# A MoE decoder kernel: the experts' pairs staggered by one and two stages on TensorE

## What is computed

```
scores = sigmoid(x @ router_w)                    # 64 experts
idx    = top 8 experts of each token, out of its 4 best groups
gate   = scores[idx] / sum * 2.5
for e in 64 experts:                              # D = 1024, hidden = 256
    xb = x[tokens of e]
    hb = silu(xb @ w_gate[e]) * (xb @ w_up[e])
    y[tokens of e] += (hb @ w_down[e]) * gate
y += (silu(x @ s_gate) * (x @ s_up)) @ s_down     # shared expert
x  = layer_norm(alpha * x + y)
```

## Time and profile before

| | us |
|---|---|
| median of 3 runs | 1343.61 (1341.33 to 1345.3) |
| profiled execution, its own time | 1345.01 |
| its span in the profile | 1343.2 |
| PE busy | 1307.0 (97%) |
| DVE busy | 421.1 (31%) |
| ACT busy | 307.3 (23%) |
| POOL busy | 28.1 (2%) |
| up projection L420, busy | 450.5, 2048 instructions |
| down projection L482, busy | 226.5, 992 instructions |

### The profile page before, as it was taken

How to read it: one execution, slowest core, us unless ns; L and a number is a source line. 1 busy time by engine, 2 the same in 40 slices (tenths; PEclk the granted TensorE clock), 3 DMA queues, 4 the chain that set the end, 5 groups by cost and what they waited for, 6 DMA issues and landing times.

```text
span 1343.2 us, 15738 instructions
## 1 busy us (share of the span) xinstructions
PE 1307.0 (97%) x6237; PEld 657.3 (49%) x6237; DVE 421.1 (31%) x903; ACT 307.3 (23%) x666; POOL 28.1 (2%) x101
## 2 busy tenths in 40 slices
PE   7999999999999999999989999999999999999996
PEld 5877854343443434344336655434434343444432
DVE  2767265212121211212133656421212112121213
ACT  3354331121121111111111343111211111111112
POOL 1004000000000000000000000000000000000000
PEclk9999999999999999999999998999999999999998
DMA  9306056789999999999983618588999999999991
GB/s 340 130 15 246 1 205 274 320 329 436 411 439 412 434 424 425 437 412 435 421 313 142 251 63 345 213 319 338 429 424 435 414 428 431 414 431 420 433 418 80
DMA packets 40581, 446.24 MB, mean 332 GB/s; under 512 B 5928, under 2 KB 8411, under 8 KB 23131
## 3 DMA queue, kind: packets, MB, share of 16 engines
q1 hardware_dynamic: 40006, 445.23, 80.0%
q10 hardware_dynamic: 532, 0.43, 0.1%
HBM read 444.60 MB, written 1.05 MB: 332 GB/s over the span
## 4 chain that ended last, share of the span: by engine, by line
PE 95%; DVE 2%; ACT 1%; issue 0%; DMA 0%; SPq 0%; DVEq 0%
PE psum L420 33%; PE psum L482 17%; PE psum L474 10%; PE psum L433 9%; PE psum L2047 4%; PE psum L2189 4%; PE psum L1167 3%; PE psum L574 2%; PE psum L1610 2%; PE psum L459 1%; PE psum L2195 1%; PE psum L1456 1%; PE psum L1206 1%; PE psum L607 1%; PE psum L466 1%; PE psum L568 1%
## 5 line engine op out<-in xcount | busy, mean ns | idle before, releaser
L420 PE MATMUL psum<-w_up_ring,moe_x_selected 128*64 128x512 f32 x2048 | 450.5, 592 | 0.0
L420 PEld LDWEIGHTS psum<-w_up_ring,moe_x_selected 128*64 128x64 f32 x2048 | 146.8, 137 | 290.4 <-issue 290.4
L482 PE MATMUL psum<-w_down_ring,moe_hT 128*64 128x512 f32 x992 | 226.5, 598 | 0.0
L1017 DVE SCALAR_TENSOR_TENSOR moe_h<-moe_silu,moe_slot_gate,psum 128x256 f32<-128x256 f32 x64 | 30.8, 480 | 381.3 <-ACT moe_silu L784 381.3
L482 PEld LDWEIGHTS psum<-w_down_ring,moe_hT 128*64 128x64 f32 x992 | 65.7, 136 | 128.5 <-issue 128.3
L784 ACT ACTIVATE moe_silu<-psum 128x256 f32<-128x256 f32 x64 | 24.7, 385 | 405.9 <-PE psum L420 405.9
L1022 DVE TENSOR_TENSOR moe_out_low<-psum,moe_out_high 128x512 fp32r<-128x512 f32 x64 | 44.3, 692 | 232.5 <-ACT moe_out_high L796 232.5
L474 PE MATMUL psum<-moe_out_high,moe_matchT 128*128 128x512 f32 x256 | 113.8, 444 | 0.0
L433 PE MATMUL psum<-moe_match,moe_x_high 128*128 128x448 f32 x256 | 102.3, 400 | 0.0
L474 PE MATMUL psum<-moe_out_low,moe_matchT 128*128 128x512 f32 x256 | 101.4, 396 | 0.0
L433 PE MATMUL psum<-moe_match,moe_x_low 128*128 128x448 f32 x256 | 93.2, 364 | 0.0
(11 more groups left out here) (500 smaller groups left out, 1124.7 us busy)
## 6 DMA issues: line engine op xcount, KB each, us to landing
w_up_ring<-in_moe_up SPq DMA_DIRECT2D x60, 4096.0 KB, 15.1
w_down_ring<-in_moe_down SPq DMA_DIRECT2D x62, 2048.0 KB, 13.2
w_up_ring<-in_moe_up SPq DMA_DIRECT2D x8, 2048.0 KB, 11.4
w_up_ring<-in_ev_w_in SPq DMA_DIRECT2D x4, 2048.0 KB, 13.2
w_up_ring<-in_od_w_in SPq DMA_DIRECT2D x4, 2048.0 KB, 12.7
w_up_ring<-in_ev_w_out SPq DMA_DIRECT2D x2, 2048.0 KB, 8.0
moe_shared_weights<-in_shared_up SPq DMA_DIRECT2D x2, 2048.0 KB, 7.7
moe_w_down_extra<-in_moe_down SPq DMA_DIRECT2D x2, 2048.0 KB, 18.0
```

What stands on the lines that cost most here:

```text
L420: last = nc.tensor.matmul(k.psum[e * SLOTS:(e + 1) * SLOTS, 6, :], xsel[:, kk, own:own + SLOTS], up_view(slots[e], kk), start=kk == 0, sto ...
L482: last = nc.tensor.matmul(k.psum[e * SLOTS:(e + 1) * SLOTS, bank, :], hT[:, j * P + e * SLOTS:j * P + (e + 1) * SLOTS], places[e][:, j, ha ...
```

## The change

The stage of pair p on TensorE becomes: up of pair p; match turn if i is 0 or 2; gather if i is 3; the whole combine of pair p-2 (8 matmuls in one row); down of pair p-1; turn of pair p. The transposes write PSUM bank 5 in place of bank 7. ACT and DVE read the down projection's result one stage later too (`take_high(p - 1)`, `take_low(p - 1)`). The down weights are asked for in the order of their new use. In `first_two_pairs` the shared expert's transposes go to bank 3 and no longer wait for `low`; the combine of pair 0 and the down of pair 1 move into the stage of pair 2. At the end the combine of pair 30 and the down of pair 31 are added after the last stage, and both parts of the shared expert's last product stand before the combine of pair 31. The matmuls are the same in number and shape. The overflow path (taken only when an expert has more than 56 tokens) keeps its own order, with its transposes still in bank 7; its hunk is left out below.

```diff
-    def pe_turn():
+    def pe_turn(bank=5):
 
         for j in range(KF):
-            last = nc.tensor.transpose(turn_ps[:, j * P:(j + 1) * P], h[:, j * P:(j + 1) * P], k.ident[:])
+            last = nc.tensor.transpose(k.psum[:, bank, j * P:(j + 1) * P], h[:, j * P:(j + 1) * P], k.ident[:])
...
-        def refill_down(p, i, par, freed):
+        def refill_down(pair, par, freed):
             sp.wait_ge(s.down_b, freed)
-            load_down_pair(sp, k.w_down_both[:, 2 * par:2 * par + 2], d, layer, 2 * i + par, dn[par])
...
         refill_up(2, 1, 0)
         refill_up(3, 1, 1)
-        refill_down(3, 1, 1, 2)
+        refill_down(4, 0, 1)
         refill_up(4, 2, 0)
-        refill_down(4, 2, 0, 1)
+        refill_down(3, 1, 2)
         refill_up(5, 2, 1)
-        refill_down(5, 2, 1, 4)
         with sp.Fori(3, PAIRS // 2) as i:
-            for par in range(2):
-                refill_up(2 * i + par, i, par)
-                refill_down(2 * i + par, i, par, 2 * i + par - 1)
+            refill_up(2 * i, i, 0)
+            refill_down(2 * i - 1, 1, 2 * i - 2)
+            refill_up(2 * i + 1, i, 1)
+            refill_down(2 * i, 0, 2 * i - 1)
+        refill_down(PAIRS - 1, 1, PAIRS - 2)
...
             shared_up(1, range(2, KD)).then_inc(s.shared_up, 1)
+            pe.wait_ge(s.turned_sb, 1)
             pe_turn_match((0, 1)).then_inc(s.match_turned, 1)
-            pe.wait_ge(s.turned_sb, 1)
             pe.wait_ge(dn[0], 16)
             pe_down(k.w_down[0:2], 0, 4).then_inc(s.down_a, 1)
             pe_down(k.w_down[0:2], 1, 7).then_inc(s.down_b, 1)
             pe.wait_ge(s.shared_h, NT)
-            pe.wait_ge(s.low_a, 1)
-            pe.wait_ge(s.low_b, 1)
-            pe.wait_ge(s.matchT, 1)
             for t in range(NT):
                 for j in range(KF):
-                    last = nc.tensor.transpose(k.psum[:, 4, (t * KF + j) * P:(t * KF + j + 1) * P],
+                    last = nc.tensor.transpose(k.psum[:, 3, (t * KF + j) * P:(t * KF + j + 1) * P],
                                                sh[:, t, j * P:(j + 1) * P], k.ident[:])
             last.then_inc(s.shared_hT_psum, 1)
-            pe_combine(0, 0, begin=True)
-            pe_turn_match((2, 3)).then_inc(s.match_turned, 1)
             pe.wait_ge(s.h, 2)
+            pe.wait_ge(s.matchT, 1)
             pe_turn().then_inc(s.turned, 1)
-            pe_combine(0, 1, begin=True).then_inc(s.combined, 1)
-            pe.wait_ge(s.turned_sb, 2)
-            pe.wait_ge(dn[1], 16)
-            pe.wait_ge(s.shared_hT, 1)
-            pe_down(k.w_down[2:4], 0, 4).then_inc(s.down_a, 1)
-            pe_down(k.w_down[2:4], 1, 7).then_inc(s.down_b, 1)
 
         def pair(q, i, first=False, final=False):
 
-            p, par = 4 * q + i, i % 2
-            slots, turn = (2 * par, 2 * par + 1), 2 * q + i // 2
+
+            p, par, turn = 4 * q + i, i % 2, 2 * q + i // 2
+            slots = (2 * par, 2 * par + 1)
             if i == 0:
                 pe.wait_ge(s.xsel_a, 4 * q + 3)
                 pe.wait_ge(s.xsel_b, 4 * q + 3)
             pe.wait_ge(gu[par], 16 * (turn + 1) + 16)
             pe.wait_ge(s.h, p)
             pe_up(slots, i, 4 * q + 4 if i == 0 else None).then_inc(s.up, 1)
-            pe.wait_ge(s.low_a, p)
-            pe.wait_ge(s.low_b, p)
-            pe.wait_ge(s.matchT, 2 * q + (i + 1) // 2)
+            pe.wait_ge(s.turned_sb, p)
+            if i % 2 == 0:
+                pe_turn_match((i, i + 1)).then_inc(s.match_turned, 1)
+            pe.wait_ge(s.low_a, p - 1)
+            pe.wait_ge(s.low_b, p - 1)
             if i == 3 and not final:
                 pe.wait_ge(s.match, NT * (q + 1) + 1)
                 pe_gather(4 * (q + 1), NT * (q + 2))
                 pe.wait_ge(s.quad_gates, q + 2)
                 pe.wait_ge(s.match_bf, q + 2)
                 pe_slot_gates().then_inc(s.slot_gates, 1)
-            pe_combine((i - 1) % 4, 0)
-            if i < 2:
-                pe_turn_match((2 * i, 2 * i + 1)).then_inc(s.match_turned, 1)
-            pe.wait_ge(s.h, p + 1)
-            if i == 3 and not final:
-                pe.wait_ge(s.gates_read, q + 2)
-            pe_turn().then_inc(s.turned, 1)
-            pe_combine((i - 1) % 4, 1).then_inc(s.combined, 1)
-            if first and i == 2:
+            pe.wait_ge(s.matchT, 2 * q + i // 2)
+            begin = first and i == 2
+            if begin:
+                pe.wait_ge(s.shared_hT, 1)
+            pe_combine((i - 2) % 4, 0, begin=begin)
+            pe_combine((i - 2) % 4, 1, begin=begin).then_inc(s.combined, 1)
+            if first and i == 3:
                 pe.wait_ge(s.shared_wd, 16)
                 shared_down(0, 0)
                 shared_down(0, 1)
-            pe.wait_ge(s.turned_sb, p + 1)
-            if first and i == 2:
-                down_places = extra_down
+                places = extra_down
                 pe.wait_ge(x.dn_extra, 16)
             else:
-                down_places = [k.w_down[slot] for slot in slots]
-                pe.wait_ge(dn[par], 16 * (turn + 1) if par else 16 * turn)
+                places = k.w_down[2 - 2 * par:4 - 2 * par]
+                pe.wait_ge(dn[1 - par], 16 * (2 * q + i // 2))
             if i == 3 and not final:
                 pe.wait_ge(s.xsel_a, 4 * q + 8)
-            pe_down(down_places, 0, 4).then_inc(s.down_a, 1)
-            pe_down(down_places, 1, 7).then_inc(s.down_b, 1)
+            pe_down(places, 0, 4).then_inc(s.down_a, 1)
+            if i == 3 and not final:
+                pe.wait_ge(s.gates_read, q + 2)
+            pe_down(places, 1, 7).then_inc(s.down_b, 1)
+            pe.wait_ge(s.h, p + 1)
+            if i % 2 == 0:
+                pe.wait_ge(s.matchT, turn + 1)
+            if i == 3 and not final:
+                pe.wait_ge(s.xsel_b, 4 * q + 8)
+            pe_turn().then_inc(s.turned, 1)
 
         first_two_pairs()
         for i in range(2, 4):
...
         n_over = pe.value_load(k.over_dram[0:1, 2:3], min_val=0, max_val=MAX_OVER)
         pair(QUADS - 1, 3, final=True)
         shared_down(1, 0)
+        pe.wait_ge(s.low_a, PAIRS - 1)
+        pe.wait_ge(s.low_b, PAIRS - 1)
+        pe_combine(2, 0)
+        pe_combine(2, 1).then_inc(s.combined, 1)
+        pe.wait_ge(s.turned_sb, PAIRS)
+        pe.wait_ge(dn[1], 16 * (PAIRS // 2))
+        pe_down(k.w_down[2:4], 0, 4).then_inc(s.down_a, 1)
+        pe_down(k.w_down[2:4], 1, 7).then_inc(s.down_b, 1)
+        shared_down(1, 1)
         pe.wait_ge(s.low_a, PAIRS)
         pe.wait_ge(s.low_b, PAIRS)
         with pe.If(n_over < 1):
             for t in range(NT):
-                if t == 1:
-                    shared_down(1, 1)
                 for half in range(2):
                     pe_combine(3, t, (half,)).then_inc(s.y_ready, 1)
 
...
             take_silu(p)
             if i == 3 and not final:
                 take_selected(4 * (q + 1))
+            if i % 2 == 0:
+                take_match(q, i // 2)
+            take_high(p - 1)
             take_turned(p)
-            if i < 2:
-                take_match(q, i)
-            take_high(p)
 
         take_silu(0)
         shared_silu(0)
...
         act.wait_ge(s.table_sb, 1)
         act.dma_start(k.over_dram, table_i[:]).then_inc(s.table_dram, 16)
         take_turned(1)
-        take_match(0, 1)
-        take_high(1)
...
                 dve.wait_ge(s.slot_gates, q + 2)
                 dve.wait_ge(s.h, p + 1)
                 read_slot_gates()
-            take_low(p)
+            take_low(p - 1)
 
         gated_h(0, 0)
         shared_h(0)
...
         shared_h(1)
         take_low(0)
         dve.wait_ge(s.shared_hT_psum, 1)
-        nc.vector.tensor_copy(shT[:].rearrange("p t j c -> p (t j c)"), k.psum[:, 4, :]).then_inc(s.shared_hT, 1)
-        take_low(1)
+        nc.vector.tensor_copy(shT[:].rearrange("p t j c -> p (t j c)"), k.psum[:, 3, :]).then_inc(s.shared_hT, 1)
...
                 pair(q, i)
         for i in range(4):
             pair(QUADS - 1, i, final=True)
+        take_low(PAIRS - 1)
```

More of the change, by code:

```diff
@@ L510, in sync @@
         load_down_pair(sp, extra_down_both[:], d, layer, 2, x.dn_extra)
-        def refill_down(p, i, par, freed):
+        def refill_down(pair, par, freed):
             sp.wait_ge(s.down_b, freed)
-            load_down_pair(sp, k.w_down_both[:, 2 * par:2 * par + 2], d, layer, 2 * i + par, dn[par])
+            load_down_pair(sp, k.w_down_both[:, 2 * par:2 * par + 2], d, layer, pair, dn[par])
         refill_up(2, 1, 0)
         refill_up(3, 1, 1)
-        refill_down(3, 1, 1, 2)
+        refill_down(4, 0, 1)
         refill_up(4, 2, 0)
-        refill_down(4, 2, 0, 1)
+        refill_down(3, 1, 2)
         refill_up(5, 2, 1)
-        refill_down(5, 2, 1, 4)
         with sp.Fori(3, PAIRS // 2) as i:
-            for par in range(2):
-                refill_up(2 * i + par, i, par)
-                refill_down(2 * i + par, i, par, 2 * i + par - 1)
+            refill_up(2 * i, i, 0)
```

(6 more changed lines are left out.)

## The result

The changed kernel takes 1356.65 us (median of 4 runs, 1355.54 to 1359.42), the kernel before 1343.38 (1341.33 to 1345.3): 13.3 us slower, ratio 1.0101, 95% interval 1.0087 to 1.0116. Forecast were 1364, 20 us slower, range 1354 to 1369. The direction and the mechanism held; the forecast size was half as large again as the measured one.

The account below looks back on a forecast made before the run. TensorE's own row was taken as the bound, busy in all 250 us of the middle window. The terms +21.0 - 1.0 - 3.4 + 3.4 gave +20.0 us, so 1364 us counted from the median, range 1354 to 1369.

Parts of the forecast that it names:

- second round trip, 60 stages: Transposes alone between down and up add one more half-to-full-to-half array shape change per stage: 0.35 us each, +21.0 us.
- match turn directly behind the up: First full-array work after an up, 15 times a layer: taken as 0, with 3 us either way.
- wait for `h` gone: Transposes no longer stall for `h` in stages i = 2, 8 times a layer: -1.0 us.
- first pairs' wait gone: Shared expert's transposes no longer wait for `low` of pair 0: 1.7 us a layer, -3.4 us in all.
- end of the layer: Four more matmuls of 0.43 stand ahead of the layer norm's start: +1.7 us a layer, +3.4 us.
- the combine's 0.105: Extra time of the first combine matmul behind an up, weights not loaded ahead; assumed for the lone transposes too.
- My own second reading, from the transposes' side: Transposes cost 0.565 us between down and up against 0.23 in the combine: difference 0.335, against 0.35 by borders.
- B: Half price: transposes' weights load under the drain, only two borders count, 0.195 us a stage; 1354.3 us, chance 0.07.
- A: The forecast itself, extra round trip at 0.35 us a stage: 1364 us, own range 1359 to 1368, chance 0.80.
- C: Faster: short transposes pass between down and up for nothing, removed stalls remain; 1339.2 us, chance 0.05.
- D: No change: the weights' queue is the true bound and absorbs PE's extra time; 1343.6 us, chance 0.05.
- E: Worse: longer idle at the layers' border keeps the clock low longer, or a late landing; about 1369 us, chance 0.03.

Follow-up runs that it names:

- turn_in_row: The changed kernel with the two transposes moved from behind the down projection to directly behind the combine; 1341.25 us, ratio 0.9978 to the kernel before.
- match_front: The kernel before with the match turn moved from inside the combine to directly behind the up, stages i = 0 and 1; 1340.24 us, ratio 0.9982.
- first_wait_back: The changed kernel with the shared expert's transposes in the first pairs waiting for `low` of pair 0 again; 1360.07 us (one run).
- tail_late: The changed kernel with the shared expert's last part back between the halves of the last combine; 1355.01 us (one run).
- turn_halves: The changed kernel, order untouched, with the transposes done as four 64-column products with the identity; 1354.06 us, ratio 1.008 to the kernel before.
- turn_twice: The changed kernel with the transposes done an extra time between the two halves of the down projection; 1388.99 us (one run).

## Why the prediction was right, and where its size was off

By its own steps, each in microseconds over both layers:

| step | forecast | measured | from |
|---|---|---|---|
| second round trip, 60 stages | +21.0 | +17.9 | turn_in_row, 8.66 a layer for 29 of the 30 |
| match turn directly behind the up | 0 (bounds 3 either way) | -2.6 | match_front, 1.23 a layer for 14 of the 15 |
| wait for `h` gone | -1.0 | about -1.4 | read in stages i = 2, 0.09 x 16 |
| first pairs' wait gone | -3.4 | -2.9 | first_wait_back |
| end of the layer | +3.4 | +3.6 | tail_late |
| sum | +20.0 | +14.6 | the traces: +13.9 |

Most of the 6 us missed lie in the first two rows. The steps measured one by one come to 0.7 us more than the two layers grew by. In the stages of a whole quad they do add up: 4 x 0.30 - 2 x 0.09 - 0.09 = 0.93, where a quad grew by 60.03 - 59.09 = 0.94. So the 0.7 lies in the first and last stages of the layers, where no run isolates it.

**The round trip.** What I got right are its borders: 0.10 to leave down (0.11 measured), 0.05 in the up behind, read directly in the changed trace and gone when the shape stays (turn_halves). What I mis-sized is the first weight load of the transposes. I took the combine's 0.105; the lone transposes take 0.37 to the up where those with weights loaded ahead took 0.31, so only 0.06. My own second reading, from the transposes' side, had already given 0.335, and I chose the larger of the two. The price is 0.30 and not 0.35: 0.045 of the difference is this load, the rest rounding and the choice of reading.

**The match turn.** It was in the bounds, and I took the middle, 0. A row that pointed there was in my group: the first combine matmul behind transposes lasts 0.31 and behind an up 0.34. It could have told 0.03 of the 0.09. That short bf16 matmuls right after a border hide part of what the first f32 weights cost there is my reading of these rows; match_front shows that the place counts, and not why. A round trip has one first matmul, and it matters which.

**The wait for `h`.** In stage i = 2 of before the combine with its transposes took 442.25 - 439.89 = 2.36, in i = 3, where `h` is long ready behind the gather, 2.27, by PE's timeline of before:

```profile
401.18 0.50 PE L474 MATMUL psum<-moe_out_high,moe_matchT 128*128 128x512 f32 x1
...
403.45 3.65 PE L482 MATMUL psum<-w_down_ring,moe_hT 128*64 128x512 f32 x16
```

That is 0.09, not 0.06. This is read from the trace, no run isolates it; the stages without a match turn, 12.73 in turn_in_row against 12.81 in before, give 0.08.

**The rivals.** B needed both borders and nothing for the weights, 1354.3. The measured 1356.65 is nearer to B than to A, yet not for B's reason: the round trip costs 0.30, nearer to A's 0.35 than to B's 0.195, because the weights are exposed, by a little over half. What brings the whole down to B's number is the match turn, which neither of them counted; without it the time would be about 2.6 us higher, in A's range. The stated range reached down to 1354 only for B, so that it held is in part luck. C is refuted by turn_twice, D by PE's full window and the gains of turn_in_row, which a bound by the weights' queue would have swallowed. The low clock at the layers' border lasts 6.8 us as before, so E did not come in this execution:

```profile
707.30:714.10 6.80, 5.58 (x16) 4.43 (x17) 6.18 (x10) 1.47 (x3) 0.00 (x0) 0.50 1.05 394
```

That is not enough to refute its mechanism. With the long wait at the border (4.8 us) the clock stays at 0.50 for 6.8 us in five profiles and for 10.2 in one (first_wait_back), with the short wait (3.1) for 6.8 in three and 3.4 in one (match_front): too few to tell the wait's doing from scatter. E's price lies behind the first residual and so outside the lengths above.

## What to carry to other kernels

Where TensorE is full, count the changes of array shape in the hand-written order before anything else: here two tiny transposes cost 0.24 us in a row of their own shape and 0.53 between two products in halves, and a reordering that removes real waits can still lose by it. Keep full-array work together, try the shortest work first behind a border (0.09 us a stage here), and read the layer's end separately: the 1.7 us of products ahead of the first residual were paid in full, and behind it they were free, because PE waits 3.1 us for DVE there. When two readings of the same price differ, carry both into the sum.

## What the runs showed of the hardware that I had not expected

- The same transposing costs 0.43 us as four f32 products in halves (eight records) and 0.22 us for half of it; two transposes of the full shape cost 0.24 in the row. Doing it as ordinary f32 products takes 0.19 us more than the transposes in the row, and that eats up most of what the saved borders bring.
- Behind a border from halves, the two 128x128 transposes took 0.06 us more than in the row (0.37 against 0.31), the first 128x128 f32 matmul of the combine 0.105 more (0.34 against 0.235). I read both as weights that are not loaded ahead.
